# A two-block transformer on one NeuronCore: the recurrence's work dealt out anew among VectorE, ScalarE, GpSimd and TensorE

## What is computed

```python
def rg_lru(xc, wa, ba, wx, bx, lam, reverse):
    r = sigmoid(einsum("bshi,hij->bshj", xb, wa) + ba)     # 8 blocks of 64 channels
    i = sigmoid(einsum("bshi,hij->bshj", xb, wx) + bx)
    log_a = LRU_C * r * log_sigmoid(lam)
    a = exp(log_a)
    mult = sqrt(-expm1(2.0 * log_a))                       # 1 at the first position
    b = mult * i * xf
    h = scan(h = a * h_before + b)                         # over the sequence, reverse or not
    return h

def first_block(x, ...):
    z = rms_norm(x, norm1_g) @ w_in
    q, k, v, xr, yr = split(z)
    attn_out = block_attention(axial_rope(q), axial_rope(k), v)
    xc = depthwise_conv(xr, lru_conv_w, lru_conv_b, 2, 1)  # 4 taps
    h_fwd = rg_lru(xc, ..., reverse=False)
    h_bwd = rg_lru(xc, ..., reverse=True)
    lru_out = (h_fwd + h_bwd) * gelu(yr)
    x = x + concatenate([attn_out, lru_out]) @ w_out
    h = rms_norm(x, norm2_g)
    ...
```

## Time and profile before

| what | value |
|---|---|
| device time, median of 3 runs | 3763.79 us (3762.78 to 3765.53) |
| the profiled execution's own time | 3762.5 us |
| its span, first to last instruction | 3760.7 us |
| mean granted TensorE clock | 0.973 of full speed |
| TensorE busy (matmuls) | 3515.1 us, 93% of the span |
| VectorE busy | 1766.0 us, 47% |
| ScalarE busy | 1351.0 us, 36% |
| GpSimd busy | 681.9 us, 18% |
| share of the chain that ended last | TensorE 81%, VectorE 12%, ScalarE 4% |

### The profile page before, as it was taken

One profiled execution on the slowest core, in us unless ns is written; L12 is line 12 of the kernel. 1 busy time (PEld: TensorE's weight loads), 2 busy tenths in 40 slices (PEclk: granted clock), 3 DMA queues, 4 the chain that ended last, 5 costly groups with the idle time before them and its releaser, 6 DMA issues.

```text
span 3760.7 us, 43653 instructions
## 1 busy us (share of the span) xinstructions
PE 3515.1 (93%) x17204; PEld 2827.1 (75%) x17204; DVE 1766.0 (47%) x1726; ACT 1351.0 (36%) x1540; POOL 681.9 (18%) x280
## 2 busy tenths in 40 slices
PE   5899787999999987999999999999889899999997
PEld 3677666888888866888877777777657688888885
DVE  6876944322313347232267888888544321111114
ACT  5687713423412334322233444444341232132112
POOL 1100321222222211111121111111112112222221
PEclk9999898999999998999999999999999999999998
DMA  2000111111111112111111111111112111111112
GB/s 104 23 1 18 67 56 34 50 45 50 48 47 50 45 45 79 39 34 39 39 45 40 40 39 39 38 35 39 45 51 95 40 39 50 49 46 50 47 48 73
DMA packets 43275, 174.91 MB, mean 47 GB/s; under 512 B 4800, under 2 KB 4800, under 8 KB 41920
## 3 DMA queue, kind: packets, MB, share of 16 engines
q1 hardware_dynamic: 43200, 173.84, 14.2%
HBM read 161.24 MB, written 12.58 MB: 46 GB/s over the span
## 4 chain that ended last, share of the span: by engine, by line
PE 81%; DVE 12%; ACT 4%; issue 2%; DMA 0%; POOL 0%; DVEq 0%; ACTq 0%; SPq 0%
PE ps L340 68%; DVE conv_acc L1169 2%; PE ps L362 2%; PE ps L1483 2%; PE ps L1495 2%; PE ps L1472 1%; PE ps L1650 1%; PE ps L1637 1%; DVE small L1209 1%; PE ps L1644 1%; DVE conv_acc L1171 1%; PE ps L1589 1%; PE ps L1623 1%; PE ps L355 1%; DVE h_lo_part L433 1%
## 5 line engine op out<-in xcount | busy, mean ns | idle before, releaser
L340 PE MATMUL ps<-h_hi_part,w_hi_part 128*128 128x512 f32 x3504 | 1119.9, 401 | 121.1 <-DVE h_lo_part L433 71.1
L317 POOL TENSOR_TENSOR w_lo_part<-w_raw,w_hi_part 128x1024 fp32r<-128x1024 f32 x272 | 668.1, 2456 | 3034.8 <-ACT w_hi_part L310 3034.3
L340 PE MATMUL ps<-h_lo_part,w_hi_part 128*128 128x512 f32 x3504 | 1089.1, 392 | 0.0
L340 PE MATMUL ps<-h_hi_part,w_lo_part 128*128 128x512 f32 x3504 | 1087.5, 392 | 0.0
L340 PEld LDWEIGHTS ps<-h_hi_part,w_hi_part 128*128 128x128 f32 x3504 | 649.7, 190 | 284.2 <-issue 127.4
L310 ACT ACTIVATE w_hi_part<-w_raw 128x1024 fp32r<-128x1024 f32 x272 | 288.0, 1059 | 1516.8 <-PE ps L340 1444.8
L340 PEld LDWEIGHTS ps<-h_lo_part,w_hi_part 128*128 128x128 f32 x3504 | 663.0, 189 | 141.6
L340 PEld LDWEIGHTS ps<-h_hi_part,w_lo_part 128*128 128x128 f32 x3504 | 662.7, 189 | 141.5
L1169 DVE SCALAR_TENSOR_TENSOR conv_acc<-u_pad,cols,conv_acc 128x1024 f32<-128x1024 f32 x232 | 307.4, 1325 | 20.3 <-DVE conv_acc L1169 2.6
L1069 DVE TENSOR_TENSOR residual<-residual,ps 128x1024 f32 x56 | 68.4, 1222 | 389.4 <-PE ps L340 389.0
L340 PE MATMUL ps<-u_lo,w_hi_part 128*128 128x512 f32 x736 | 226.6, 389 | 0.0
(11 more groups left out here) (325 smaller groups left out, 3471.4 us busy)
## 6 DMA issues: line engine op xcount, KB each, us to landing
w_raw<-in_w SPq DMA_DIRECT2D x272, 512.0 KB, 3.5
residual<-in_x SPq DMA_DIRECT2D x4, 1024.0 KB, 9.9
residual<-in_x SPq DMA_DIRECT2D x2, 2048.0 KB, 7.2
...
residual_again<-residual_spill SPq DMA_DIRECT2D x1, 4096.0 KB, 14.4
...
```

What stands on the lines that cost most here:

```text
L317: pool.tensor_tensor(WLO[:, slot], WRAW[:, slot], f32(WHI[:, slot]), ALU.subtract).then_inc(w_ready, 1)
L340: last = pe.matmul(PS[:, ps, b * HALF:(b + 1) * HALF], st[:, slot, k, :], mv[:, k, b * HALF:(b + 1) * HALF], start=(k == 0 and n == 0), st ...
```

## The change

It has five parts, all in the recurrence or at its two ends.

1. The gate job of tile 0 no longer stands behind attention on TensorE: its four parts are put into the last rounds and the last product (`gate_pe`), and their four tanh on ScalarE between the copies there (`gate_tanh_act`).
2. ScalarE's square roots of a tile move behind the exponentials and the high part of the next input.
3. The decay, a VectorE instruction for each tile and direction, becomes a ScalarE instruction with scale -2 and bias -1 (`decay_act`). For the second direction it stands behind the next tile's gate tanh.
4. The lower parts of the weights of jobs 9 to 19 are made by VectorE (`split_rest`), in the middle of its own program, instead of by GpSimd; a gate job's high and lower parts cover its four used parts alone.
5. The lower parts of `MIX` 0 to 6 are made by VectorE ahead of the last scan; GpSimd makes none. ScalarE's decay of the last direction stands between its high parts 6 and 7.

The diff without the semaphores' declarations and the initial setting of the constant -1:

```diff
-        def split_act(act, jp, slot):
+        def split_act(act, jp, slot, nk=KT):
...
-            act.activation(WHI[:, slot], WRAW[:, slot], ACT.Copy).then_inc(w_hi, 1)
+            act.activation(WHI[:, slot, 0:nk], WRAW[:, slot, 0:nk], ACT.Copy).then_inc(w_hi, 1)
+        def parts(j):
+            return len(J_GATE) if j in J_GATE else KT
+        def split_rest(eng, j):
+            slot, ks = j % 2, slice(0, parts(j))
+            eng.wait_ge(w_hi, j + 1)
+            eng.tensor_tensor(WLO[:, slot, ks], WRAW[:, slot, ks], f32(WHI[:, slot, ks]), ALU.subtract).then_inc(w_ready, 1)
...
         def gpsimd_program(pool):
-            splits_pool(pool, 0, J_OUT + 2)
+            splits_pool(pool, 0, J_GATE[0] + 1)
+            split_rest(pool, J_GATE[0] + 1)
+            pool.wait_ge(w_ready, J_OUT + 2)
...
-            for k in range(4):
-                pool.wait_ge(h_hi, 8 * GEN_MIX + k + 1)
-                pool.tensor_tensor(LO[:, k, :], MIX[:, k, :], f32(HI[:, k, :]), ALU.subtract).then_inc(h_ready, 1)
-                pool.wait_ge(h_ready, 8 * GEN_MIX + k + 1)
...
+        def gate_tanh_act(act, t, m):
+            if m < 3:
+                act.wait_ge(gate_done, 3 * t + m + 1)
+            else:
+                act.wait_ge(job_done, J_GATE[t] + 1)
+            act.activation(TH[t % 2][m][:, :], psl(2 + m % 2), ACT.Tanh, scale=0.5,
+                           bias=small(HB + 4 * m + t)).then_inc(gate_evac, 1)
@@ att_act @@
+                if g == 62:
+                    gate_tanh_act(act, 0, 0)
+                if g == 63:
+                    gate_tanh_act(act, 0, 1)
+                    gate_tanh_act(act, 0, 2)
             out(3)
+            gate_tanh_act(act, 0, 3)
...
             def split_next(j):
-                split_act(act, j // 2 + 1, j % 2)
+                split_act(act, j // 2 + 1, j % 2, parts(j + 2))
+            def decay_act(t, d):
+                act.wait_ge(lru_inv, 2 * t + d + 1)
+                act.wait_ge(lru_sqrt, 2 * t + d + 1)
+                act.activation(TH[t % 2][2 * d][:, :], LY[t % 2][d][:, :], ACT.Identity, bias=small(MINUS1), scale=-2.0
+                               ).then_inc(lru_decay, 1)
@@ gates_act @@
-                for m in range(4):
...
+                if t:
+                    for m in range(4):
+                        gate_tanh_act(act, t, m)
                 split_next(J_GATE[t])
+                if t:
+                    decay_act(t - 1, 1)
...
-                for d in range(2):
-                    act.activation(LS[a][d][:, :], TH[a][2 * d][:, :], ACT.Sqrt)
...
                 if t < 3:
                     xc_hi_act(t + 1)
+                for d in range(2):
+                    act.activation(LS[t % 2][d][:, :], TH[t % 2][2 * d][:, :], ACT.Sqrt).then_inc(lru_sqrt, 1)
+                decay_act(t, 0)
                 yr_act(t)
             act.wait_ge(job_done, J_OUT)
-            split_h_act(act, MIX, GEN_MIX, lambda k: act.wait_ge(lru_done, max(k - 3, 0) + PRIMED))
+            for k in range(KT - 1):
+                mix_hi_act(k)
+            decay_act(3, 1)
+            mix_hi_act(KT - 1)
...
             def conv(t):
+                split_rest(dve, J_GATE[t])
...
@@ scan @@
-                st.do(dve.scalar_tensor_tensor(y[:, :], e[:, :], -2.0, y[:, :], ALU.add, ALU.mult))
+                dve.scalar_tensor_tensor(y[:, :], e[:, :], -2.0, y[:, :], ALU.add, ALU.mult).then_inc(lru_inv, 1)
+                dve.wait_ge(lru_inv, n)
                 if d == 0 and t < 3:
                     xc_lo_dve(dve, t + 1)
-                st.do(dve.scalar_tensor_tensor(p[:, :], p[:, :], -1.0, y[:, :], ALU.add, ALU.mult))
+                if d and t == 3:
+                    split_rest(dve, J_OUT + 1)
+                    split_h_dve(dve, MIX, GEN_MIX, 0, KT - 1)
+                dve.wait_ge(lru_sqrt, n)
                 st.do(dve.scalar_tensor_tensor(s[:, :], s[:, :], -1.0, y[:, :], ALU.mult, ALU.mult))
...
                 st.do(dve.tensor_tensor(i[:, :], i[:, :], s[:, :], ALU.mult))
+                if d == 0 and t < 3:
+                    split_rest(dve, J_YR[t] + 2)
+                dve.wait_ge(lru_decay, n)
                 st.do(dve.tensor_tensor_scan(y[:, way], p[:, way], i[:, way], 0.0, ALU.mult, ALU.add))
+            dve.wait_ge(w_ready, J_GATE[0] + 2)
             for t in range(4):
                 inputs(t)
+                split_rest(dve, J_GATE[t] + 2)
...
-            dve.wait_ge(h_ready, 8 * GEN_MIX + 4)
-            split_h_dve(dve, MIX, GEN_MIX, 4)
+            split_h_dve(dve, MIX, GEN_MIX, KT - 1)
...
+        def gate_pe(pe, t, m):
+            j = J_GATE[t]
+            if m == 0:
+                pe.wait_ge(w_ready, j + 1)
+                pe.wait_ge(xc_lo, t + 1)
+            if 4 * t + m < 2:
+                pe.wait_ge(e_done, 63 + m)
+            else:
+                pe.wait_ge(gate_evac, 4 * t + m - 1)
+            three_pass(pe, 2 + m % 2, WHI[:, j % 2, m, :], WLO[:, j % 2, m, :], XCH, XCL
+                       ).then_inc(gate_done if m < 3 else job_done, 1)
@@ att_pe @@
                 turn(g)
+                if g >= 62:
+                    gate_pe(pe, 0, g - 62)
                 if g >= 2:
                     pv(g // 2 - 1, range(4 * (g % 2), 4 * (g % 2) + 4))
+            gate_pe(pe, 0, 2)
             pv(31, range(QT))
+            gate_pe(pe, 0, 3)
```

31 lines of the change are left out of this document (11 added, 20 removed).

## The result

| | before | changed | ratio, 95% interval |
|---|---|---|---|
| median of 5 runs, us | 3762.78 (3759.02 to 3765.53) | 3740.57 (3737.63 to 3744.47) | 0.9942 [0.9927, 0.9956] |
| profiled execution, us | 3762.5 | 3737.63 | |
| its span, us | 3760.7 | 3735.8 | |

The changed kernel takes 22.2 us less; 3741 was predicted.

A forecast was written before the change was run, and what follows sets the result against it. VectorE was taken to bound the recurrence, lengthened by GpSimd beside it. Job 20 starting 24.8 us earlier, less 1.9 for the clock, gave 22.9 off 3762.5: 3739.6, or 3741 as median; range 3733 to 3752.

The forecast's parts named there:

- the conv's start: VectorE's first conv tap: 356.0 instead of 357.3, as the weights' high part no longer waits behind ScalarE's roots.
- VectorE's sum: VectorE's work from conv's start to the last product: 109.3 us instead of 128.7, before new waits.
- 13 long rows: VectorE instructions from 357.31 on, each about 2.05 us over normal beside GpSimd's lower parts; 26.7 us to go.
- New waits: In the recurrence, VectorE's waits for ScalarE and TensorE: 5.4 us in all, ends 0 and 10.
- under 1.2 us in any one place: Sign expected in the changed profile: the limit on VectorE's waiting at any one place.
- first rival: ScalarE and TensorE set the recurrence's pace: waits of 10 us, low clock in all three tiles; 3749 us, chance 0.13.
- The projection's start: Job 20 of the output projection starts at 482.8 instead of 507.64, 24.8 us earlier, before the clock charge.
- the clock's charge: TensorE's gate matmuls run at the lower clock after a gap; 1.9 us charged, for one tile.
- The sum: Gain up to job 20: 24.8 less 1.9 for the clock, 22.9 us; nothing behind it changes.
- The long rows stay: Something other than GpSimd lengthens VectorE's rows, so 26.7 us come back; 3760 us, no difference; chance 0.05.
- The lower level for the recurrence: TensorE falls to its lower clock in three tiles of the recurrence, 63 us on the path; 3804 us, chance 0.03.
- second rival: VectorE's lengthened recurrence rows remain because GpSimd is not their cause; 3760 us, chance 0.05.

The follow-up runs named there:

- a1: Changed kernel with tile 0's gates and their tanh behind attention again: 3737.53 us, 0.9932 of the kernel before.
- a2: Changed kernel with ScalarE's square roots ahead of the logarithms and exponentials again: 3739.76 us, 0.9939 of the kernel before.
- b3: Changed kernel plus 22 unused GpSimd additions, each reading two SBUF operands of 512 columns: 3752.6 us, 0.9974 of the kernel before.
- b1: Changed kernel with MIX lower parts 0 to 3 on GpSimd and the other four on VectorE behind the last product: 3744.95 us, 0.9959 of the kernel before.
- b4: Changed kernel plus 22 unused GpSimd memsets of 512 columns, which only write: 3739.68 us, 0.994 of the kernel before.
- b5: Changed kernel with GpSimd again making the recurrence weights' lower parts and the first four of MIX: 3756.79 us, 0.9983 of the kernel before.
- c1: Changed kernel with two of VectorE's weight lower parts moved, ahead of the second direction and its scan: 3738.73 us, 0.9934 of the kernel before.
- c4: Changed kernel with two weight lower parts moved on VectorE and the output projection's start reordered: 3734.64 us, 0.9922 of the kernel before.

## Why the prediction was right

**Part 1** was taken at 0.3 us; 0.26 in a1.

**Part 2, the conv's start.** Predicted 356.0, measured 356.56 in a run whose A lies 0.3 later: 1.1 us of gain relative to A, 1.3 predicted. The working left out what a2 shows, the 2.4 us of exponentials in tile 3, since it compared only with the kernel before, where VectorE's chain was too long to wait there.

**Parts 3 to 5, VectorE's sum.** From 356.56 to 473.26 are 116.7 us. Of them VectorE waits 7.5 (the waits above without the 6.7 and 0.4 that lie ahead of 356.56); its own work is 109.2, predicted 109.3. The terms without a row were taken at 0.65 and 1.1 us and measured 0.69 and 1.14. All 13 long rows went, and b3 shows that reading by GpSimd is their cause.

**New waits** is the mis-sized term: 7.5 instead of 5.4. The high part of the job behind `yr` came 1.38 and 1.34 us late in tiles 1 and 2 (0.34 in tile 0), not 0.2 to 1.0, the decay 1.0, not 0.7. From conv's end to the second decay's end ScalarE's chain took 15.9 us in tile 0, where 15.8 were predicted, but 17.0 in tile 1. That is also why the line "under 1.2 us in any one place" was wrong. Its cause is in the chain: a tile's pace of 30.5 us is one turn through VectorE, TensorE and ScalarE. TensorE's wait of 0.9 us for VectorE's lower part in tiles 1 and 2, ahead of the job that this high part stands behind, isn't in the working. The first rival's mechanism is thus there, at a price inside my range.

**The projection's start.** M to J was predicted at 12.1 and measured 11.6, so job 20 started at 484.85; the forecast with the clock's charge was 482.8 + 1.9 = 484.7. The charge of **1.9 for the clock** did not fall in this profile: the gates after the gap of 2.01 us at 370.29 ran at full clock. It cancelled the 2.1 us missing under New waits. That the two agree is luck of this profile: in others the charge does fall, as 1.5 us in tile 0 of a1, b1 and b4, and in up to three tiles (b5, c1, c4).

**The sum** up to job 20 was 22.9 us, measured 507.64 - 484.85 = 22.8. Nothing behind it changed up to N: J to N is 71.81 and 71.93. The profiled executions differ by 24.9 us, the medians by 22.2; the 2.2 us of the former that lie behind N are within the scatter there.

**What the sum hid.** It came out right as a whole, but its terms are not what each part is worth. By the sum's terms, part 4 takes away the nine long rows that stand beside lower parts of weights in the kernel before, some 18 us, for 9.4 us of its own work, 9 us in all; undone alone it costs 1.05, or nothing at the same clock. Part 5 undone costs 7.0 from M to N, both together 15.1. Parts 1 to 3 alone give 7.9.

**Rivals.** *The long rows stay* is refuted: none did. *The lower level for the recurrence* did not come: the clock is 1.00 in the three windows above, and no profile of an edited kernel has it under 0.77 in them. The Trainium skill ("Perfetto Trace Analysis", Optimizing Scalar/DVE Operations) says that with DVE saturated, offloading some work to Scalar or even GPSIMD may make sense, but that between GPSIMD and DVE it might not help, because of a shared SBUF read port. The prediction set its first half beside the second rival's time, 3760; the measured 3740.57, b1 and b5 go against that half and with the caveat. Part 3, work given to ScalarE, agrees with it.
